# RWKV chunk matrices as 64x64 blocks in two quadrants of the array

## The chip, the cores and the metric

The kernel runs on one core of one Trainium2 chip. The metric is the device time of one execution in microseconds, the median of several runs. One program computes the whole network.

## The reference, cut to what matters

Four layers follow each other: an RG-LRU layer and a sparse-attention layer, each with an MLP, and then, in `second_block`, a layer with differential attention and RWKV-7 side by side and a retention layer, each with two SwiGLU blocks. There are 512 tokens of 1024 features. The change is in the RWKV-7 half of the third layer: eight heads of 64, a recurrence over the tokens.

```
def rwkv7_recurrence(r, w, k, v, kk, a):
    def step(state, inp):
        r_t, w_t, k_t, v_t, kk_t, a_t = inp
        sa = jnp.einsum('bhvk,bhk->bhv', state, -kk_t)
        state = (state * w_t[:, :, None, :]
                 + sa[..., None] * (kk_t * a_t)[:, :, None, :]
                 + v_t[..., None] * k_t[:, :, None, :])
        return state, jnp.einsum('bhvk,bhk->bhv', state, r_t)
```

The result is normalised by head, a bonus `sum(r*k*r_k) * v` is added, and the sum is gated.

## The kernel before, in words

The tokens are cut into 8 chunks of 64. In a chunk the recurrence is a 64x64 triangular system per head. The kernel works on pairs of heads, p = 0 to 3 (128 features, two heads h of 64 rows). Every engine runs its own fixed list of instructions (`rwkv_pe`, `rwkv_act`, `rwkv_pool`, `rwkv_dve`); they meet at counting semaphores. A `Steps` object names the steps of one pair: `done` counts one up, `wait` waits for a named step of pair p. `fr_*` are the steps of the front of a pair, `bk_*` those of its back.

The work of a pair, in order. **Front elementwise work** (`dve_front_0` to `dve_front_7`, `act_front_*`, and the full-width matmuls kk, w, a, g and bonus of 512 columns) makes decayed keys and queries. It is done for pair p+1 between the levels of pair p. **Turns**: four transposes by TensorE, 128x128 each, times four tensors. **Matrices** (`pe_mats`, `dve_mats`): five products of 64 rows deep per head, masked by VectorE on the way out of PSUM. A tile of 128x128 holds two chunks; only its two diagonal 64x64 blocks are in use, the mask clears the others. Four tiles j make the 8 chunks, so each matrix is 128x512. **Levels** (`pe_level_u`, `pe_level_d`): the triangular matrix is inverted by doubling, in five levels l. The matrix D and its transpose DT are both kept. In each level, for each head, U = Gb'D (line 2096), ScalarE copies U out of PSUM (line 2293), then DT'U and U'DT (lines 2109 and 2110), and VectorE adds them to D and DT (lines 2447 and 2448). GpSimd prepares the masked Gb for the next level (line 2350). In level 5 only DT is still wanted. **Back** (`pe_back`): P = DT'RHS, copied out by ScalarE (head 0) and VectorE (head 1, line 2462), then the products QT, Y1, MT and N. **Scan** (`pe_scan`): seven steps that carry the state from chunk to chunk; each waits for VectorE's add of the step before (line 2480). **Normalisation**: VectorE adds the scan's part (line 2488), mean (line 2167), subtraction (line 2495), square on ScalarE (line 2321), variance (line 2172), logarithm and exponential on ScalarE (lines 2323 and 2325), and three elementwise steps on VectorE (lines 2499 to 2501). The matrices of the next pair are made around these.

After the normalisation VectorE scales the next pair's keys (`dve_front_0`, line 2366) and ScalarE squares them (line 2231). In ScalarE's list this square stands ahead of the first U copy of the new pair. In the last pair no front work is left; the first output matmuls (`pe_out_part`, lines 304 to 306) are put between the steps of its scan.

## Time and profile before

| | before |
|---|---|
| median of 3 runs | 3835.3 us (3829.93 to 3839.46) |
| the profiled execution | 3837.58 us, of which the span is 3835.7 us |
| TensorE matmul busy | 3623.7 us, 94% of the span |
| VectorE busy | 1989.1 us, 52% |
| ScalarE busy | 1228.4 us, 32% |
| GpSimd busy | 532.7 us, 14% |
| granted TensorE clock, mean | 0.975 |
| RWKV stage | about 1926 to 2205 us of the span |

A float32 matmul appears in the trace as two records, and its weight load as two; counts of records are therefore twice those of the program's matmuls. A row that says "x16" is 16 records. The duration in a row is that of a record from start to modelled end, so the pace of a stream is read from the starts. A clock of 1.00 is 2.4 GHz, 0.50 is 1.2 GHz.

### The profile page before, as it was taken

The numbers are of one execution on the slowest core, as the hardware profiler recorded it, in microseconds if no ns is written. First come the engines' busy times: TensorE is split into PE (matmuls) and PEld (weight loads), VectorE is DVE, ScalarE is ACT, GpSimd is POOL, SyncE is SP. The second block draws the span as 40 slices with busy tenths as digits, with TensorE's granted clock in tenths as the row PEclk, the third lists the DMA queues.
The fourth block names the chain that finished last, engine by engine and source line by source line (L and its number), as shares of the span: only waits on it lengthen the run. The fifth ranks groups of instructions, "written<-read, shape, count | busy, mean of one in ns | idle before, by whom it ended". The sixth has DMA issues, their size and how long they took to land.

```text
span 3835.7 us, 44975 instructions
## 1 busy us (share of the span) xinstructions
PE 3623.7 (94%) x17279; PEld 2899.5 (76%) x17279; DVE 1989.1 (52%) x2747; ACT 1228.4 (32%) x1651; POOL 532.7 (14%) x398
## 2 busy tenths in 40 slices
PE   6999999899999999998998889999999899989998
PEld 5788888546888788876777768887888677767887
DVE  6555563464555554455566444446444433345445
ACT  3632232464322322233223132224222322233222
POOL 1220010010000221110132121112111100012111
PEclk8999999899999999999999999999999999989999
DMA  3233234001232232221200023232223222222231
GB/s 103 86 102 105 91 95 106 20 1 34 88 104 93 86 97 92 98 87 45 72 12 1 1 77 99 98 98 68 97 98 98 77 77 80 85 66 79 97 98 66
DMA packets 232517, 295.37 MB, mean 77 GB/s; under 512 B 21893, under 2 KB 201464, under 8 KB 232392
## 3 DMA queue, kind: packets, MB, share of 16 engines
q1 hardware_dynamic: 230864, 290.48, 24.0%
q0 software_dynamic: 1152, 3.05, 0.4%
q8 instruction: 85, 1.39, 0.2%
q14 instruction: 40, 0.33, 0.0%
q10 hardware_dynamic: 376, 0.12, 0.0%
HBM read 291.53 MB, written 2.10 MB: 77 GB/s over the span
## 4 chain that ended last, share of the span: by engine, by line
PE 82%; DVE 8%; ACT 4%; POOL 3%; issue 2%; POOLq 0%; ACTq 0%; DMA 0%; DVEq 0%
PE bank L304 23%; PE bank L306 22%; PE bank L305 22%; POOL tmp L636 1%; PE bank L333 1%; PE bank L335 1%; PE bank L334 1%; PE bank L2074 1%; ACT h_hi L550 1%; PE bank L2579 1%; PE bank L2110 1%; DVE x L681 1%; ACT whi L294 1%; DVE wlo L300 1%; DVE h_lo L665 1%
## 5 line engine op out<-in xcount | busy, mean ns | idle before, releaser
L304 PE MATMUL bank<-h_hi,whi 128*128 128x512 f32 x2800 | 1114.3, 398 | 57.2 <-DVE h_lo L665 38.2
L305 PE MATMUL bank<-h_lo,whi 128*128 128x512 f32 x2800 | 1101.8, 393 | 0.0
L306 PE MATMUL bank<-h_hi,wlo 128*128 128x512 f32 x2800 | 1101.4, 393 | 0.0
L294 ACT ACTIVATE whi<-raw 128x2048 fp32r<-128x2048 f32 x273 | 521.7, 1911 | 1400.6 <-PE bank L306 1346.1
L300 DVE TENSOR_TENSOR wlo<-raw,whi 128x2048 fp32r<-128x2048 f32 x273 | 631.9, 2315 | 435.1 <-ACT whi L294 434.8
L304 PEld LDWEIGHTS bank<-h_hi,whi 128*128 128x128 f32 x2800 | 533.8, 191 | 183.0 <-issue 64.0
L305 PEld LDWEIGHTS bank<-h_lo,whi 128*128 128x128 f32 x2800 | 533.7, 191 | 115.5 <-issue 4.9
L306 PEld LDWEIGHTS bank<-h_hi,wlo 128*128 128x128 f32 x2800 | 532.9, 190 | 112.6
L304 PE MATMUL bank<-u_hi,whi 128*128 128x512 f32 x1376 | 539.4, 392 | 27.0 <-DVE wlo L300 10.6
L305 PE MATMUL bank<-u_lo,whi 128*128 128x512 f32 x1376 | 538.2, 391 | 0.0
L306 PE MATMUL bank<-u_hi,wlo 128*128 128x512 f32 x1376 | 538.1, 391 | 0.0
L304 PEld LDWEIGHTS bank<-u_hi,whi 128*128 128x128 f32 x1376 | 260.3, 189 | 85.1 <-DVE wlo L300 11.4
L445 POOL TENSOR_TENSOR tmp<-tmp,rstd 128x512 f32<-128x512 f32 x88 | 175.5, 2015 | 1065.3 <-ACT tmp L414 1065.0
L305 PEld LDWEIGHTS bank<-u_lo,whi 128*128 128x128 f32 x1376 | 260.3, 189 | 54.1
L306 PEld LDWEIGHTS bank<-u_hi,wlo 128*128 128x128 f32 x1376 | 260.0, 189 | 54.3
L499 DVE TENSOR_TENSOR fsum<-fsum,bank 128x512 f32<-128x512 f32 x352 | 235.5, 686 | 92.6 <-PE bank L306 92.5
L499 DVE TENSOR_TENSOR x<-x,bank 128x512 f32<-128x512 f32 x256 | 169.6, 684 | 51.0 <-PE bank L306 50.9
L480 DVE TENSOR_TENSOR tmp<-bank,tmp 128x512 f32<-128x512 f32 x88 | 60.9, 692 | 253.1 <-PE bank L306 236.3
L465 DVE TENSOR_TENSOR tmp<-bank,rstd 128x512 f32<-128x512 f32 x88 | 60.1, 691 | 216.3 <-PE bank L306 215.4
L422 ACT ACTIVATE u_hi<-tmp 128x512 fp32r<-128x512 f32 x88 | 55.7, 633 | 336.5 <-DVE tmp L480 336.5
L469 DVE SCALAR_TENSOR_TENSOR tmp<-bank,rstd 128x512 f32<-128x512 f32 x64 | 44.1, 692 | 180.8 <-PE bank L306 180.8
L426 ACT ACTIVATE tmp<-tmp 128x512 f32<-128x512 f32 x64 | 40.4, 632 | 257.2 <-DVE tmp L469 257.2
(400 smaller groups left out, 3381.2 us busy)
## 6 DMA issues: line engine op xcount, KB each, us to landing
raw<-in_ffn_wgu SPq DMA_DIRECT2D x88, 1024.0 KB, 5.1
raw<-in_ffn_wd SPq DMA_DIRECT2D x44, 1024.0 KB, 4.9
raw<-in_mlp_w_up SPq DMA_DIRECT2D x32, 1024.0 KB, 5.7
raw<-in_mlp_w_down SPq DMA_DIRECT2D x32, 1024.0 KB, 4.9
raw<-in_odd_w_in SPq DMA_DIRECT2D x24, 1024.0 KB, 5.1
raw<-in_even_w_in SPq DMA_DIRECT2D x13, 1024.0 KB, 5.3
raw<-in_rg_w_in SPq DMA_DIRECT2D x8, 1024.0 KB, 5.8
raw<-in_odd_w_out SPq DMA_DIRECT2D x8, 1024.0 KB, 5.0
```

Of the source, the lines that this page charges most:

```text
L294: e.activation(whi[:, n % 2, :], raw[:, n % 2, :], ACT.Copy).then_inc(hi_ready, 1)
L300: e.tensor_tensor(wlo[:, n % 2, :], raw[:, n % 2, :], whi[:, n % 2, :].bitcast(F32), ALU.subtract).then_inc(lo_ready, 1)
L304: pe.matmul(o, w_hi, r_hi, start=first, stop=False)
L305: pe.matmul(o, w_hi, r_lo, start=False, stop=False)
L306: return pe.matmul(o, w_lo, r_hi, start=False, stop=last)
L422: e.activation(u_hi[:, u, :], tmp[:, 2 + j, :], ACT.Copy).then_inc(uhi_done, 1)
L426: e.activation(tmp[:, 2 + j, :], tmp[:, j, :], ACT.Square)
L445: e.tensor_tensor(tmp[:, j, :], tmp[:, j, :], rstd[:, :], ALU.mult).then_inc(scaled, 1)
L465: ins = e.tensor_tensor(tmp[:, j, :], pbank[half + j][:, :], rstd[:, :], ALU.mult)
L469: ins = e.scalar_tensor_tensor(tmp[:, j, :], pbank[half + j][:, :], 0.0, rstd[:, :], ALU.max, ALU.mult)
L480: e.tensor_tensor(tmp[:, 2 + j, :], pbank[half + 2 + j][:, :], tmp[:, j, :], ALU.mult)\
L499: e.tensor_tensor(dst[:, m, :], dst[:, m, :], pbank[half + m % 4][:, :], ALU.add)\
```

## The change

The two diagonal blocks of each 128x128 tile become two matmuls of 64x64, one on rows 0 to 63 of the array with results on partitions 0 to 63 (even chunk), one on rows 64 to 127 with results on partitions 64 to 127 (odd chunk). They sit in two opposite quadrants of the array and alternate. All matrices shrink from 128x512 to 128x256, masks to 64 columns (`m_half`, cut out of the old masks once by GpSimd). `pe_mats` now works in three groups: for each chunk both heads, into one bank per head, so that all four quadrants are used; a group is signalled once. `dve_mats` takes two matrices with one instruction where they lie side by side (`m02`, `m13`). In a level, DT'U and U'DT are no longer interleaved: the one goes to banks 3 and 4 and signals D, the other goes to banks 1 and 5 and signals T; VectorE adds each after its own signal. U goes to banks 0 and 2. In `pe_back` the products QT, Y1, MT and N alternate quadrants; those of odd and even chunks land in different banks, so some copies are done in halves (`odd_even`). The scan's outputs move from bank 6 to bank 5. GpSimd now adds the identity to both heads' D before it prepares the first Gb.

```diff
+        MBANK = ((0, 2), (3, 4), (1, 7))
...
-        def hz(h, j):
-            return rz[:, 11 * h + j, :].rearrange("p (j n) -> p j n", j=QT)
-
-        MATS = [[hz(h, j) for j in range(4)] for h in HH]
-        Dm, DTm, Um, Gb, RHS, PM = ([hz(h, j) for h in HH] for j in range(5, 11))
+        def hz(h, t):
+            return rz[:, 6 * h + t, :]
+
+        def by_chunk(m):
+            return m.rearrange("p (j n) -> p j n", n=HD)
+
+        def two(t):
+            return [[by_chunk(hz(h, t)[:, i * 4 * HD:i * 4 * HD + 4 * HD]) for h in HH] for i in range(2)]
+        (M0, M2), (M1, M3), (Dm, DTm), (Um, Gb) = (two(t) for t in range(4))
+        RHS, PM = ([hz(h, t).rearrange("p (j n) -> p j n", j=QT) for h in HH] for t in (4, 5))
         QTt, MTt = rz[:, 22, :], rz[:, 23, :]
+        EE = (slice(0, HD), slice(HD, P))
...
-        def pe_mats(pe, p, k0, k1):
-            for k in range(k0, k1):
-                i, h = MORD[k]
-                r = slice(h * HD, h * HD + HD)
+        def pe_mats(pe, p, g):
+            if g == 0:
+                fr_dve.wait(pe, "tokA", p)
+                fr_act.wait(pe, "tokB", p)
+            elif g == 1:
+                fr_act.wait(pe, "tokK", p)
+                fr_dve.wait(pe, "tokV", p)
+            else:
+                fr_dve.wait(pe, "bon", p)
+            for s, i in enumerate(MGRP[g]):
                 l_, r_ = ((be, al), (be, rt_of(p)), (kt_, al), (kt_, rt_of(p)), (al, be))[i]
-                b = MBANK[k % 5]
-                if k == 0:
-                    fr_dve.wait(pe, "tokA", p)
-                elif k == 1:
-                    fr_act.wait(pe, "tokB", p)
-                elif k == 2:
-                    fr_act.wait(pe, "tokK", p)
-                elif k == 3:
-                    fr_dve.wait(pe, "tokV", p)
-                elif k == 4:
-                    fr_dve.wait(pe, "bon", p)
-                else:
-                    i0, h0 = MORD[k - 5]
-                    fr_dve.wait(pe, f"d{h0}" if i0 == 0 else f"m{i0}{h0}", p)
-                for j in range(QT):
-                    q = slice(j * P, j * P + P)
-                    ins = pe.matmul(pbank[b][:, q], l_[r, q], r_[r, q], start=True, stop=True)
-                fr_pe.done(ins, f"m{i}{h}")
+                for c in range(8):
+                    q = slice(c * HD, c * HD + HD)
+                    o_ = slice((4 * s + c // 2) * HD, (4 * s + c // 2) * HD + HD)
+                    for h in HH:
+                        ins = pe.matmul(pbank[MBANK[g][h]][EE[c % 2], o_], l_[EE[h], q], r_[EE[h], q], start=True, stop=True)
+            fr_pe.done(ins, f"M{g}")
...
         def pe_level_u(pe, p, l):
             for h in HH:
                 if l == 1:
                     fr_pool.wait(pe, f"gb1{h}", p)
-                    fr_dve.wait(pe, "m31", p)
                 else:
                     bk_pool.wait(pe, f"gb{l}{h}", p)
                     bk_dve.wait(pe, f"D{l - 1}{h}", p)
-                for j in range(QT):
-                    ins = pe.matmul(pbank[h][:, j * P:j * P + P], Gb[h][:, j, :], Dm[h][:, j, :], start=True, stop=True)
+                for c in range(8):
+                    e, j = EE[c % 2], c // 2
+                    ins = pe.matmul(pbank[2 * h][e, j * HD:j * HD + HD], Gb[h][e, j, :], Dm[h][e, j, :], start=True, stop=True)
                 bk_pe.done(ins, f"U{l}{h}")
 
         def pe_level_d(pe, p, l):
             for h in HH:
                 if l == 1:
                     fr_pool.wait(pe, f"DT{h}", p)
+                    fr_dve.wait(pe, "m131", p)
                     if p:
                         bk_act.wait(pe, "yln", p - 1)
+                else:
+                    bk_dve.wait(pe, f"T{l - 1}{h}", p)
                 bk_act.wait(pe, f"U{l}{h}", p)
-                for j in range(QT):
-                    q = slice(j * P, j * P + P)
-                    if l < 5:
-                        pe.matmul(pbank[2 + h][:, q], DTm[h][:, j, :], Um[h][:, j, :], start=True, stop=True)
-                    ins = pe.matmul(pbank[4 + h][:, q], Um[h][:, j, :], DTm[h][:, j, :], start=True, stop=True)
-                bk_pe.done(ins, f"D{l}{h}")
+                for i, (l_, r_) in enumerate(((DTm, Um), (Um, DTm))):
+                    if i == 0 and l == 5:
+                        continue
+                    for c in range(8):
+                        e, j = EE[c % 2], c // 2
+                        ins = pe.matmul(pbank[((3, 4), (1, 5))[i][h]][e, j * HD:j * HD + HD], l_[h][e, j, :],
+                                        r_[h][e, j, :], start=True, stop=True)
+                    bk_pe.done(ins, f"{'DT'[i]}{l}{h}")
...
         def pe_back(pe, p):
             for h in HH:
-                bk_dve.wait(pe, f"D5{h}", p)
+                bk_dve.wait(pe, f"T5{h}", p)
                 fr_act.wait(pe, f"rhs{h}", p)
                 fr_pool.wait(pe, f"ra{h}", p)
-                for j in range(QT):
-                    ins = pe.matmul(pbank[h][:, j * P:j * P + P], DTm[h][:, j, :], RHS[h][:, j, :], start=True, stop=True)
+                for c in range(8):
+                    e, j = EE[c % 2], c // 2
+                    ins = pe.matmul(pbank[h][e, j * P:j * P + P], DTm[h][e, j, :], RHS[h][e, j, :], start=True, stop=True)
                 bk_pe.done(ins, f"P{h}")
             bk_act.wait(pe, "P0", p)
             bk_dve.wait(pe, "P1", p)
-            for h in HH:
-                for j in range(QT):
-                    ins = pe.matmul(pbank[2][h * HD:h * HD + HD, j * P:j * P + P], PM[h][:, j, HD:P],
-                                    MATS[h][1][:, j, :], start=True, stop=True)
+            if p:
+                bk_act.wait(pe, "yln", p - 1)
+            for c in range(8):
+                e, j = EE[c % 2], c // 2
+                for h in HH:
+                    ins = pe.matmul(pbank[(2, 4)[c % 2]][EE[h], c * HD:c * HD + HD], PM[h][e, j, HD:P], M1[h][e, j, :],
+                                    start=True, stop=True)
             bk_pe.done(ins, "QT")
-            for h in HH:
-                for j in range(QT):
-                    o_ = pbank[3][h * HD:h * HD + HD, j * P:j * P + P]
-                    pe.matmul(o_, tokV[:, j, h * HD:h * HD + HD], MATS[h][3][:, j, :], start=True, stop=False)
-                    ins = pe.matmul(o_, PM[h][:, j, 0:HD], MATS[h][1][:, j, :], start=False, stop=True)
+            for c in range(8):
+                e, j = EE[c % 2], c // 2
+                o_ = pbank[(3, 5)[c % 2]][:, c * HD:c * HD + HD]
+                for h in HH:
+                    pe.matmul(o_[EE[h], :], tokV[e, j, EE[h]], M3[h][e, j, :], start=True, stop=False)
+                for h in HH:
+                    ins = pe.matmul(o_[EE[h], :], PM[h][e, j, 0:HD], M1[h][e, j, :], start=False, stop=True)
             bk_pe.done(ins, "Y1")
...
-                        bk_act.done(e.activation(flat(Um[h]), pbank[h][:, :], ACT.Copy), f"U{l}{h}")
+                        bk_act.done(e.activation(flat(Um[h]), pbank[2 * h][:, 0:4 * HD], ACT.Copy), f"U{l}{h}")
...
-                fr_pool.done(e.tensor_tensor(Dm[h], Dm[h], wide(ident[:, :]), ALU.add), f"Dm{h}")
-                fr_dve.wait(e, f"m0{h}", p)
-                fr_pool.done(e.tensor_tensor(Gb[h], MATS[h][0], wide(lmask[:, 1, :]), ALU.mult), f"gb1{h}")
+                fr_pool.done(e.tensor_tensor(Dm[h], Dm[h], wide(ident2), ALU.add), f"Dm{h}")
+            for h in HH:
+                fr_dve.wait(e, f"m02{h}", p)
+                fr_pool.done(e.tensor_tensor(Gb[h], M0[h], wide(low_mask(1)), ALU.mult), f"gb1{h}")
...
-        def dve_mats(e, p, k0, k1):
-            for k in range(k0, k1):
-                i, h = MORD[k]
-                src = pbank[MBANK[k % 5]][:, :].rearrange("p (j n) -> p j n", j=QT)
-                fr_pe.wait(e, f"m{i}{h}", p)
-                if i == 4:
-                    do_fr(e, e.tensor_tensor(Dm[h], src, wide(m_low), MUL), f"m4{h}", p, False)
+        def dve_mats(e, p, g):
+            fr_pe.wait(e, f"M{g}", p)
+            for h in HH:
+                src = by_chunk(pbank[MBANK[g][h]][:, :])
+                if g == 0:
+                    do_fr(e, e.tensor_tensor(Dm[h], src[:, 0:QT, :], wide(m_half[:, 2, :]), MUL), f"m4{h}", p, False)
+                elif g == 1:
+                    do_fr(e, e.tensor_tensor(by_chunk(hz(h, 0)), src, wide(m_half[:, 0, :], 8), MUL), f"m02{h}", p, False)
+                    do_fr(e, e.tensor_tensor(DTm[h], src[:, 0:QT, :], wide(low_mask(0)), MUL), f"d{h}", p, False)
                 else:
-                    do_fr(e, e.tensor_tensor(MATS[h][i], src, wide((m_up, m_upd, m_up, m_upd)[i]), MUL), f"m{i}{h}", p,
-                          False)
-                if i == 0:
-                    do_fr(e, e.tensor_tensor(DTm[h], src, wide(lmask[:, 0, :]), MUL), f"d{h}", p, False)
+                    do_fr(e, e.tensor_tensor(by_chunk(hz(h, 1)), src, wide(m_half[:, 1, :], 8), MUL), f"m13{h}", p, False)
...
-                        bk_pe.wait(e, f"D{l}{h}", p)
                         if l < 5:
-                            e.tensor_tensor(flat(Dm[h]), flat(Dm[h]), pbank[2 + h][:, :], ALU.add)
-                        do_bk(e, e.tensor_tensor(flat(DTm[h]), flat(DTm[h]), pbank[4 + h][:, :], ALU.add), f"D{l}{h}", p,
-                              False)
+                            bk_pe.wait(e, f"D{l}{h}", p)
+                            do_bk(e, e.tensor_tensor(flat(Dm[h]), flat(Dm[h]), pbank[3 + h][:, 0:4 * HD], ALU.add),
+                                  f"D{l}{h}", p, False)
+                        bk_pe.wait(e, f"T{l}{h}", p)
+                        do_bk(e, e.tensor_tensor(flat(DTm[h]), flat(DTm[h]), pbank[(1, 5)[h]][:, 0:4 * HD], ALU.add),
+                              f"T{l}{h}", p, False)
```

On TensorE, one level of the last pair (level 3 and the start of level 4). `L2096` is U, `L2109` is DT'U, `L2110` is U'DT; rz holds all matrices; the last number is partitions x columns of the result. Before:

```order
L2096 MATMUL bank0<-rz_55 128x128 [waits bk_dve,bk_pool]
L2096 MATMUL bank0<-rz_55 128x128 x3
L2096 MATMUL bank1<-rz_55 128x128 [waits bk_dve,bk_pool]
L2096 MATMUL bank1<-rz_55 128x128 x3
L2109 MATMUL bank2<-rz_55 128x128 [waits bk_act]
L2110 MATMUL bank4<-rz_55 128x128
L2109 MATMUL bank2<-rz_55 128x128
L2110 MATMUL bank4<-rz_55 128x128
...
L2109 MATMUL bank3<-rz_55 128x128 [waits bk_act]
L2110 MATMUL bank5<-rz_55 128x128
```

The same level after the change; `L2103` is U, `L2121` both products:

```order
L2103 MATMUL bank0<-rz_55 64x64 [waits bk_dve,bk_pool]
L2103 MATMUL bank0<-rz_55 64x64 x7
L2103 MATMUL bank2<-rz_55 64x64 [waits bk_dve,bk_pool]
L2103 MATMUL bank2<-rz_55 64x64 x7
L2121 MATMUL bank3<-rz_55 64x64 [waits bk_act,bk_dve]
L2121 MATMUL bank3<-rz_55 64x64 x7
L2121 MATMUL bank1<-rz_55 64x64 x8
L2121 MATMUL bank4<-rz_55 64x64 [waits bk_act,bk_dve]
L2121 MATMUL bank4<-rz_55 64x64 x7
L2121 MATMUL bank5<-rz_55 64x64 x8
```

24 matmuls of 128 columns become 48 of 64 columns, in six runs of 8, and the two products of a head stand behind each other instead of alternating.

On VectorE, the adds of the same level and the next. Before, with one wait per head:

```order
L2447 TENSOR_TENSOR rz_55<-rz_55,bank2 128x512 [waits bk_pe]
L2448 TENSOR_TENSOR rz_55<-rz_55,bank4 128x512
L2447 TENSOR_TENSOR rz_55<-rz_55,bank3 128x512 [waits bk_pe]
L2448 TENSOR_TENSOR rz_55<-rz_55,bank5 128x512
L2447 TENSOR_TENSOR rz_55<-rz_55,bank2 128x512 [waits bk_pe]
```

After the change:

```order
L2467 TENSOR_TENSOR rz_55<-rz_55,bank3 128x256 [waits bk_pe]
L2470 TENSOR_TENSOR rz_55<-rz_55,bank1 128x256 [waits bk_pe]
L2467 TENSOR_TENSOR rz_55<-rz_55,bank4 128x256 [waits bk_pe]
L2470 TENSOR_TENSOR rz_55<-rz_55,bank5 128x256 [waits bk_pe]
L2467 TENSOR_TENSOR rz_55<-rz_55,bank3 128x256 [waits bk_pe]
```

The four adds stay in their order; each has half the columns and waits for its own product.

## Rows read from the trace of the kernel before

**Rows 1.** The page: the chain that ended last, share of the span by engine.
```profile
PE 82%; DVE 8%; ACT 4%; POOL 3%; issue 2%; POOLq 0%; ACTq 0%; DMA 0%; DVEq 0%
```
**Rows 2.** Busy by stretch: PE, PEld, DVE, ACT, POOL, then clock, DMA share, GB/s.
```profile
1929.50:2205.00 275.50, 245.97 (x2307) 212.10 (x2306) 160.54 (x278) 72.09 (x130) 76.17 (x64) 0.98 0.01 4
```
**Rows 3.** One level of the last pair, 2144 to 2151, in order of time.
```profile
2144.43 0.69 DVE L2447 TENSOR_TENSOR rz<-rz,bank 128x512 f32<-128x512 f32 x1 [3.10 <-PE bank L2110]
...
2146.01 1.06 PE L2096 MATMUL bank<-rz 128*128 128x128 f32 x8
2146.22 0.69 DVE L2447 TENSOR_TENSOR rz<-rz,bank 128x512 f32<-128x512 f32 x1 [0.50 <-PE bank L2110]
2146.82 0.68 DVE L2448 TENSOR_TENSOR rz<-rz,bank 128x512 f32<-128x512 f32 x1
2147.11 0.60 ACT L2293 ACTIVATE rz<-bank 128x512 f32<-128x512 f32 x1 [3.87 <-PE bank L2096]
...
2147.65 1.13 PE L2096 MATMUL bank<-rz 128*128 128x128 f32 x8 [0.58 <-DVE rz L2448]
...
2150.60 0.69 DVE L2447 TENSOR_TENSOR rz<-rz,bank 128x512 f32<-128x512 f32 x1 [3.10 <-PE bank L2110]
```
**Rows 4.** Quadrant matmuls of the back (L2138) and one scan step.
```profile
1977.93 0.69 PE L2138 MATMUL bank<-fsum,rz 64*64 64x64 f32 x32
...
1981.74 0.34 PE L2161 MATMUL bank<-tmp,rz 64*64 64x64 f32 x4
1981.91 0.29 PE L2162 MATMUL bank<-rz,tmp 64*64 64x64 f32 x4
```
**Rows 5.** VectorE and ScalarE durations by width.
```profile
L2480 DVE TENSOR_TENSOR tmp<-bank,tmp 128x64 f32<-128x64 f32 x24 | 5.4, 225 | 24.4 <-PE bank L2162 23.9
...
1999.64 0.38 ACT L2277 ACTIVATE rz<-bank 128x256 f32<-128x256 f32 x1 [3.11 <-PE bank L2083]
```
**Rows 6.** Second pair: start of level 2, of P, VectorE's front work, end of scan.
```profile
2009.48 2.05 PE L2096 MATMUL bank<-rz 128*128 128x128 f32 x16
...
2034.20 2.05 PE L2119 MATMUL bank<-rz 128*128 128x128 f32 x16
...
2024.62 1.29 DVE L2378 TENSOR_SCALAR tmp<-tmp 128x512 f32<-128x512 f32 x1
...
2027.21 1.58 DVE L2380 TENSOR_TENSOR tmp<-tmp 128x512 f32<-128x512 f32 x1
...
2050.49 0.62 DVE L2488 TENSOR_TENSOR tmp<-tmp,bank 128x448 f32<-128x448 f32 x1 [0.43 <-PE bank L2162]
```
**Rows 7.** From the end of the first pair's scan to the second pair's first level.
```profile
1986.62 0.62 DVE L2488 TENSOR_TENSOR tmp<-tmp,bank 128x448 f32<-128x448 f32 x1 [0.43 <-PE bank L2162]
...
1995.18 0.69 ACT L2323 ACTIVATE tmp<-bank,eps 128x512 f32<-128x512 f32 x1 [2.99 <-PE bank L2172]
1995.90 0.63 ACT L2325 ACTIVATE tmp<-tmp 128x512 f32<-128x512 f32 x1
...
1999.22 0.74 DVE L2499 SCALAR_TENSOR_TENSOR tmp<-tmp,par 128x512 f32<-128x512 f32 x1
...
2001.51 1.58 DVE L2366 TENSOR_SCALAR tmp<-arena,par 128x512 f32<-128x512 f32 x1
...
2003.80 1.12 PE L2007 MATMUL bank<-tmp,arena 128*128 128x512 f32 x2 [1.46 <-ACT tmp L2231]
```
**Rows 8.** Groups by line and shape: VectorE's masked copies of the matrices.
```profile
L2423 DVE TENSOR_TENSOR rz<-bank,arena 128x512 f32<-128x512 f32 x32 | 21.1, 687 | 5.9 <-PE bank L2074 5.8
```
**Rows 9.** Granted clock around the fall in the last pair's scan.
```profile
2160.00:2170.00 10.00, 7.92 (x157) 6.80 (x154) 3.33 (x12) 4.88 (x10) 0.00 (x0) 0.96 0.02 4
2170.00:2175.00 5.00, 3.97 (x21) 2.69 (x22) 0.82 (x2) 0.00 (x0) 0.00 (x0) 0.50 0.00 0
...
2180.00:2185.00 5.00, 3.22 (x19) 2.42 (x20) 1.43 (x4) 0.00 (x0) 0.00 (x0) 1.00 0.00 0
```
**Rows 10.** Scan steps of the last pair at either clock (VectorE's add).
```profile
2170.85 0.23 DVE L2480 TENSOR_TENSOR tmp<-bank,tmp 128x64 f32<-128x64 f32 x1 [2.87 <-PE bank L2162]
...
2175.40 0.23 DVE L2480 TENSOR_TENSOR tmp<-bank,tmp 128x64 f32<-128x64 f32 x1 [3.73 <-PE bank L2162]
...
2182.82 0.22 DVE L2480 TENSOR_TENSOR tmp<-bank,tmp 128x64 f32<-128x64 f32 x1 [2.21 <-PE bank L2162]
...
2185.86 0.23 DVE L2480 TENSOR_TENSOR tmp<-bank,tmp 128x64 f32<-128x64 f32 x1 [2.22 <-PE bank L2162]
```

107 lines of the change are left out of this document (58 added, 49 removed).

## The prediction

> **What bounds the kernel now.** The chain that ended last is to be read first: 82% of it is TensorE [rows 1]. But most of that is the big projections, which the change leaves alone. What counts is the RWKV stage, 275.5 us long [rows 2]. There TensorE shows 246 us busy at a clock of 0.98, VectorE 161, ScalarE 72 and GpSimd 76. So the stage is bound by TensorE, with waits in between, and nobody else is near.
>
> Then the order of time within one level [rows 3]. The first head's add to D comes at 2144.43 and again at 2150.60: a level of the last pair, which has no front work beside it, takes 6.17 us. TensorE's stream fills it: a run of 8 records (4 matmuls of 128 columns) starts every 0.89 us if nothing stands between (8 times 0.112), and a level has six such runs, 5.35 us. The rest is the wait of the second U for VectorE's add (idle 0.58). The reader is to see that ScalarE's copy of U has long idled (3.87 us) when its matmuls come.
>
> **What a run of eight 64x64 matmuls costs.** The trace has such matmuls. In the back, 32 records in four quadrants take 0.69 us to the modelled end of the last [rows 4]; less the 0.22 of that last one, they start within 0.47 us. That is 8 per quadrant, 0.058 us apart. Two opposite quadrants, with results in one bank, are what the scan uses: each head's matmul has its own half of rows and of partitions. Its 4 records take 0.34 us to the end and the next group starts 0.17 us after them [rows 4]. One after the other in a single file they would start over 3 times 0.058, 0.17 us, and end at 0.40; in two quadrants they start over 0.12 and end at 0.34. So they run side by side. A run of 8 matmuls has 16 records, 8 per quadrant: 0.47 us instead of 0.89. The bounds: 0.47, if pairs run side by side, and 0.94 if they don't. I take 0.47.
>
> The row shows two opposite quadrants writing one bank together. The Trainium skill, page "TensorEngine Tiling (Array Packing)", section "Gotcha 1: PSUM Pressure", says that different row tiles cannot access the same PSUM bank simultaneously. By that rule a run would be 0.94 us and the levels would gain nothing on TensorE; the scan's rows speak against it.
>
> **VectorE, ScalarE, GpSimd.** A VectorE instruction of 64 columns takes 0.225 us [rows 5], one of 512 columns 0.687 [rows 8]: 1.03 ns a column. So 256 columns take 0.42, and follow each other every 0.34 instead of every 0.60 [rows 3]. ScalarE's copy of 256 columns takes 0.38 [rows 5] instead of 0.60. GpSimd's instructions halve too; with 76 us busy in the stage [rows 2] I cost them at nothing, hidden beside TensorE's runs, and if that cover went they would add at most 0.7 us a level.
>
> **The sum at full clock, by stage.**
> (a) A level without front work. U starts; its result is with ScalarE 0.67 us later (0.41 for the last start, 0.22 to its end, 0.04 to hand over); the copy takes 0.38 and TensorE starts 0.34 after it (an estimate; the wait behind VectorE in [rows 3], from 2147.50, the end of its add, to 2147.65, is 0.15 and the low end, which would give 3.1); then come four runs, 1.88. Sum 3.3 instead of 6.17, 2.9 less. VectorE's four adds (1.4 us) fit in. Last pair, levels 2 to 5: 4 times 2.9, 11.6.
> (b) Levels 2 to 5 with front work, up to P. Before, 2009.48 to 2034.20, 24.7 us [rows 6]. After: level 2 has six runs and a full-width matmul, 2.8 and 0.86, so 3.7; level 3 the same; behind level 3 VectorE makes the decays, from 2024.62 to 2028.79, 4.2 us [rows 6], and with four adds (1.4) this is 5.6, longer than TensorE's part, so VectorE sets level 4; level 5 has four runs and hand-overs, 3.7. Sum 16.7, 8.0 less, three times: 24.
> (c) From the end of the scan to level 2 of the next pair. Before, 1986.62 to 2009.48, 22.9 us [rows 6, 7], with the matrices in between. VectorE's part of these shrinks from 12 instructions at 0.60, 7.2 us, to 4 at 0.60 and 4 at 0.34, 3.8 us; TensorE's from 80 records at 0.112, 9.0 us, to 160 records in four quadrants at 0.0146, 2.3 us. What is left is a chain that nothing shortens: y and mean 2.2 (0.62, a 512-column matmul 1.12 [rows 7], hand-overs), subtraction, square and variance 2.9, logarithm and exponential (0.69 [rows 7] and about as much) 1.9, three elementwise steps of 0.74 [rows 7] 2.4, the scaling of the next keys 1.58 [rows 7] and 0.1, the square 0.7, the first U copy with hand-over 0.7, four runs 1.9, the matmul w 0.9. Sum 15.3, 7.6 less, three times: 23. The stall moves: before, TensorE waits 1.46 us for the square (L2231) [rows 7]; now it has its matrices early and waits some 5 us there.
> (d) P to the end of the scan: 2034.20 to 2050.49, 16.3 us [rows 6]. QT and Y1 fall from 48 records at 0.112 to 96 records in four quadrants at 0.0146, from 5.4 to 1.4 us, but VectorE's front work (10 instructions of 0.6 behind the last add) then holds P's copy and QT's add: I take 2 less, bounds 0 and 4.0. Three times 6, and 3 in the last pair.
> (e) The first pair's matrices and level 1, by (a) and (c): 3.4 on VectorE, rhs 0.9, level 1 2.9: 7.
> Sum 11.6 + 24 + 23 + 9 + 7 = 75 us.
>
> **The clock.** In the last pair's scan the engine does a few 64x64 matmuls and six 512-column ones per step and waits between; from 2170 the clock is 0.50, by 2180 1.00 again [rows 9]. A step takes 4.55 us at the low level (2170.85 to 2175.40) and 3.04 at the high one (2182.82 to 2185.86) [rows 10]. The changed kernel thins out its work the same way in three places of every pair: the 5 us hole of (c), the hole of some 2 us where VectorE makes the decays, and all levels, in which now one half of the array at most is at work. At the low level six runs take 5.6 us instead of 2.8, so a level 2.7 us more. I count two and a half such levels a pair in the first three, 20 us, and 5 in the last: 25. Bounds: 0 if the clock holds, 100 if it never rises (below). Net 75 - 25 = 50: against the profiled execution 3837.6 - 50 = 3788. That run lies 2.3 above the median of those shown, so I say 3786.
>
> On this the Trainium skill, page "TensorE: Matmul & The Clock Gate", section "What's actually happening", says that the throttled state is the default and that activity releases it. Idle stretches before a fall are what [rows 9] show too; by the rule alone the holes of (c) would bring the low level in every pair, which is why the forecast counts it and the clock that holds is a rival.
>
> **Rivals.**
> The clock holds. For it: through the earlier scans, with 64x64 matmuls between transposes, the stage's mean stayed at 0.98 [rows 2]. Time 3837.6 - 75 = 3763. Chance 0.22.
> Opposite quadrants with one bank go one after the other, the rule above. Levels, rhs and P then stay as they are on TensorE; VectorE's shorter instructions, the matrices and QT, Y1 leave about 35 at full clock (7.6 and 2 three times, 7), less some 12 for the clock: 3815. For it only that the scan's groups are short (two matmuls a head), so that it may show less than it seems. Chance 0.1.
> Slower: the low clock stays through the stage. TensorE streams at full clock some 32 us in a pair of about 46 (28 runs of 0.47, P 1.7, matrices and the back 5.1, transposes 3.4, seven 512-column matmuls 6, scan 1.6). Doubled, that adds up to 32 less what hides beside VectorE's chains, 25 a pair: 100 in all against 75. Time 3863; it decides from 75 us of clock cost on. Against it: each back and each scan has full-width transposes and dense quadrants, after which the clock would rise. Chance 0.06.
> Nothing to measure: several gains fall behind chains that I read too short. 3835, chance 0.06.
>
> **How the numbers follow.** The forecast, the clock low for part of each pair, has 0.56 and its own range 3768 to 3808. The whole range, 3756 to 3820, takes in the clock that holds and the single file; the two last cases are outside. A measurement here can tell about 0.3%, 11.5 us, from no change. Faster by more: 0.56, 0.22, 0.1 and a little of the rest, 0.9. Within: 0.04. Slower: 0.06.
>
> **What the next profile would show.** Right: L2103 and L2121 in runs of 16 records that start within 0.47 us at clock 1.00 (0.94 proves the single file); DVE adds of 0.42 us; levels of the last pair 3.3 us apart at full clock; an idle of TensorE of about 5 us for the square's line; in the stage a mean clock of 0.75 to 0.9. A clock near 0.98 there means 3763; one near 0.6 means that the gain is gone. The prediction is wrong if the stage (275.5 us) is not 215 to 240 us long.

## The result, and the profile after

The changed kernel takes 3767.7 us (median of 4 runs, 3767.1 to 3770.4), the kernel before 3832.6 (median of 4): ratio 0.9829, 95% interval 0.9812 to 0.9846, or 65 us less. The forecast was 3786 with a range of 3756 to 3820. So the direction held, the time lies in the range, and the gain is 15 to 20 us larger than forecast. The profiled executions compare 3835.7 with 3766.3 us of span, 69.4 less.

All of it comes from the RWKV stage. The two ends that can be found in both traces are VectorE's first copy of transposed keys (L2409 before, L2429 after) and the last pair's y (L2488, L2512). Of before:

```profile
1927.51 1.28 DVE L2409 COPY fsum<-bank 128x512 f32<-128x512 f32 x2
...
2188.75 0.62 DVE L2488 TENSOR_TENSOR tmp<-tmp,bank 128x448 f32<-128x448 f32 x1 [2.07 <-PE bank L2162]
```

and of the changed kernel:

```profile
1931.80 1.28 DVE L2429 COPY fsum<-bank 128x512 f32<-128x512 f32 x2
...
2119.49 0.62 DVE L2512 TENSOR_TENSOR tmp<-tmp,bank 128x448 f32<-128x448 f32 x1 [2.08 <-PE bank L2179]
```

261.2 us have become 187.7, that is 73.5 less. From y to the end of the span it is 1646.9 against 1646.8 us. The missing 4.3 us lie ahead of the stage, in code that the change doesn't touch: there the stage begins 4.3 us later. In the twelve further profiles below it begins anywhere from 1928.3 to 1936.6. So 4.3 us is within the spread from execution to execution; but there is only one profile of the kernel before, and it begins earlier than all the others, so that the change has no part in it is not shown.

The busy time of that stretch (windows: PE, PEld, DVE, ACT, POOL, then the granted clock), before and after, to be held against [rows 2]:

```profile
1927.50:2188.80 261.30, 233.09 (x2256) 201.97 (x2254) 156.60 (x274) 69.22 (x125) 76.17 (x64) 0.98 0.02 5
```
```profile
1931.80:2119.50 187.70, 152.13 (x3790) 119.96 (x3790) 117.59 (x262) 59.81 (x129) 50.86 (x64) 0.95 0.03 8
```

The chain that ended last keeps its shares ([rows 1] had 82% for TensorE):

```profile
PE 81%; DVE 8%; ACT 4%; POOL 3%; issue 2%; POOLq 0%; ACTq 0%; DMA 0%; DVEq 0%
```

In the stage TensorE's busy time falls by 81 us, VectorE's by 39; the clock is a little lower, 0.95.

A level of the last pair, which has no front work, in order of time (of after, as [rows 3]):

```profile
2082.30 0.42 DVE L2467 TENSOR_TENSOR rz<-rz,bank 128x256 f32<-128x256 f32 x1 [1.29 <-PE bank L2121]
...
2083.47 1.13 PE L2103 MATMUL bank<-rz 64*64 64x64 f32 x32
...
2084.17 0.85 ACT L2311 ACTIVATE rz<-bank 128x256 f32<-128x256 f32 x2 [2.26 <-PE bank L2103]
...
2084.70 2.08 PE L2121 MATMUL bank<-rz 64*64 64x64 f32 x64
2085.42 0.42 DVE L2467 TENSOR_TENSOR rz<-rz,bank 128x256 f32<-128x256 f32 x1 [1.29 <-PE bank L2121]
```

From one D add to the next it is 3.12 us where it was 6.17. Two runs of U, 32 records, show 1.13 us to the end of the last, and four runs of products, 64 records, 2.08; less 0.22 for that last one, a run of 16 records starts within 0.46 to 0.47 us. That is the pace that the forecast took, and not the single file's 0.94.

The second pair (of after, as [rows 6, 7]):

```profile
1973.81 0.62 DVE L2512 TENSOR_TENSOR tmp<-tmp,bank 128x448 f32<-128x448 f32 x1 [0.43 <-PE bank L2179]
...
1980.49 1.10 PE L2103 MATMUL bank<-rz 64*64 64x64 f32 x32
1985.20 2.08 PE L2023 MATMUL bank<-tmp,arena 128*128 128x512 f32 x2 [3.60 <-ACT tmp L2249]
1987.20 2.55 PE L2121 MATMUL bank<-rz 64*64 64x64 f32 x64
...
1990.74 1.15 PE L2103 MATMUL bank<-rz 64*64 64x64 f32 x32
...
2002.97 1.34 PE L2103 MATMUL bank<-rz 64*64 64x64 f32 x32 [0.89 <-DVE rz L2467]
...
2006.05 1.96 PE L2132 MATMUL bank<-rz 64*64 64x128 f32 x32 [0.49 <-DVE rz L2470]
```

End of scan to level 2 is 16.9 us (22.9 before), level 2 to P 15.3 (24.7 before). TensorE has finished the first level's U at 1981.6 and then waits 3.60 us for ScalarE's square (L2249) ahead of the matmul of line 2023: the hole of the forecast, at 3.6 where it said 5.

The granted clock behind that hole, in the levels behind it, in the last pair's scan and in the last pair's levels:

```profile
1984.90:1988.30 3.40, 3.10 (x22) 1.60 (x24) 0.00 (x0) 0.79 (x3) 0.16 (x1) 0.50 0.00 0
...
1988.30:2003.00 14.70, 13.70 (x346) 11.01 (x343) 9.74 (x19) 8.35 (x17) 5.62 (x6) 1.00 0.01 3
...
2097.50:2107.70 10.20, 7.75 (x36) 5.20 (x36) 1.87 (x6) 3.39 (x7) 0.00 (x0) 0.50 0.00 0
...
2077.20:2089.00 11.80, 11.45 (x352) 10.85 (x352) 6.31 (x17) 3.06 (x8) 4.87 (x7) 1.00 0.02 4
```

The clock is low for 3.4 us behind the hole and back at 1.00 in the levels, where TensorE is busy over 90% of the time with half of the array. In the whole stage it is at 0.50 in three such stretches of 3.4 us, two of them behind the hole (second and third pair) and one in the first pair's scan, and in one of 10.2 us in the last pair's scan, which the kernel before has too ([rows 9]). The forecast wanted a stage mean of 0.75 to 0.9 and has 0.95.

### The profile page after: what moved, and what is told of

It is laid out like the page before. It is cut to its first block, busy times and chain, and to the rows that moved or that the text cites. A ratio compares the mean times of both kernels' runs of the same rounds, so it can differ in the third digit from the quotient of the medians.

```text
span 3766.3 us, 48073 instructions
## 1 busy us (share of the span) xinstructions
PE 3548.0 (94%) x18815; PEld 2819.5 (75%) x18815; DVE 1949.7 (52%) x2735; ACT 1218.9 (32%) x1655; POOL 506.6 (13%) x400
## 4 chain that ended last, share of the span: by engine, by line
PE 81%; DVE 8%; ACT 4%; POOL 3%; issue 2%; POOLq 0%; ACTq 0%; DMA 0%; DVEq 0%
PE bank L304 23%; PE bank L306 23%; PE bank L305 23%; POOL tmp L636 1%; PE bank L333 1%; PE bank L335 1%; PE bank L334 1%; ACT h_hi L550 1%; PE bank L2604 1%; PE bank L2121 1%; DVE x L681 1%; ACT whi L294 1%; DVE h_lo L665 1%; DVE wlo L300 1%; PE bank L1281 1%
## 5 line engine op out<-in xcount | busy, mean ns | idle before, releaser
L304 PEld LDWEIGHTS bank<-u_hi,whi 128*128 128x128 f32 x1376 | 260.5, 189 | 84.1 <-DVE wlo L300 10.6
L469 DVE SCALAR_TENSOR_TENSOR tmp<-bank,rstd 128x512 f32<-128x512 f32 x64 | 44.1, 692 | 180.8 <-PE bank L306 180.8
```

The costliest lines, as they stand in the source:

```text
L304: pe.matmul(o, w_hi, r_hi, start=first, stop=False)
L469: ins = e.scalar_tensor_tensor(tmp[:, j, :], pbank[half + j][:, :], 0.0, rstd[:, :], ALU.max, ALU.mult)
```

## The experiments

All are the changed kernel with one edit; in the last three rows, and where long files have the hole filled, edits add up. "Stage" is the time from the first copy to the last pair's y in the profiled execution (187.7 us in the changed kernel). The kernels ran in three groups of four (1, 2, 3 in the table), each beside new runs of the kernel before, whose medians were 3831.3, 3840.5 and 3831.1. So ratios are to be compared across groups, not microseconds; their intervals are 0.0012 to 0.0022 to either side. Where two kernels are closer than that, the reading rests on the stage. The stage comes from one profile each; the kernel that was run again differs by 0.2 us there. But it holds all stretches of low clock, and these move from kernel to kernel, those in the scans too: a difference of a few us in the stage is to be read with them in mind. The order in which matmuls stand in TensorE's list is called the file here; long files are 16 records of one quadrant in a row.

| | group | median, us | ratio | stage, us |
|---|---|---|---|---|
| changed kernel | result | 3767.7 | 0.9829 | 187.7 |
| the same again | 3 | 3765.1 | 0.9825 | 187.9 |
| even chunks first | 1 | 3776.3 | 0.9848 | 198.3 |
| long files | 2 | 3809.0 | 0.9923 | 221.7 |
| long files, hole filled | 3 | 3787.5 | 0.9876 | 206.3 |
| hole filled | 2 | 3769.9 | 0.9815 | 185.8 |
| joint signals | 1 | 3773.8 | 0.9836 | 195.4 |
| one bank, one add | 1 | 3773.5 | 0.9833 | 194.4 |
| matrices head by head | 2 | 3774.7 | 0.9832 | 191.7 |
| square behind U | 1 | 3758.2 | 0.9795 | 180.8 |
| its matmul later too | 3 | 3753.1 | 0.9792 | 177.5 |
| with the scan's low parts early | 3 | 3747.9 | 0.9773 | 172.2 |
| and fillers ahead of the scans | 2 | 3750.7 | 0.9761 | 170.6 |

The first row again, beside the last group:

> The changed kernel as it is, on the chip of the next three. Every theory: 3768 us, 64 us under the kernel before on the same chip, RWKV stage 188 us from the first transposed copy to the last pair's y.

It came out at 3765.1 us, ratio 0.9825 (0.9805 to 0.9845), with the same three short low stretches and the long one.

**Even chunks first.** Do opposite quadrants work side by side, and does the order of the file matter?

```diff
-                for c in range(8):
+                for c in (0, 2, 4, 6, 1, 3, 5, 7):   # in U's runs and in both products
```

> Only the order of the eight blocks within each run of the levels is changed: even chunks first, then odd ones, so that opposite quadrants no longer alternate. Theory A (the gain of the levels comes from opposite quadrants working side by side): a run of 16 records takes 0.94 us instead of 0.47, a level of the last pair 5.6 us instead of 3.1, about 10 us more in each of the first three pairs and 12 in the last, 3810 us against 3768. Rival B (the gain comes from narrower instructions on VectorE and ScalarE): runs and time stay, 3768. Rival C (thin work lowers the clock): with a quarter of the array at work the granted clock in the levels falls to 0.50 and the time passes 3850.

Measured: 3776.3 us, ratio 0.9848 (0.9832 to 0.9864). The level of the last pair is 3.80 us, neither 3.1 nor 5.6 (VectorE's adds, two levels of the last pair):

```profile
2094.50 0.42 DVE L2467 TENSOR_TENSOR rz<-rz,bank 128x256 f32<-128x256 f32 x1 [1.65 <-PE bank L2121]
...
2098.30 0.42 DVE L2467 TENSOR_TENSOR rz<-rz,bank 128x256 f32<-128x256 f32 x1 [1.65 <-PE bank L2121]
```

The records tell why. These are the starts of U's matmuls (us behind 2092), from where the stream of head 0 is under way:

```
.223 .281 .287 .340 .394 .398 .452 .456 .511 .569 .575 .627
```

One quadrant takes a new record every 0.058 us. The other quadrant's stream begins while three records of the first are still to come (pairs such as .281/.287, .394/.398, .452/.456), so each half run begins 0.287 us behind the last, five records and not eight. A run takes 0.575 us: six of them are 0.65 more than 6 times 0.467, and the level has grown by 0.68. So TensorE starts matmuls of another quadrant beside the ones ahead of them, here some three records deep. Theory A is right in kind (the order decides, at unchanged widths), but not at its price of 0.94 us a run; B falls. The clock in the last pair's levels is 1.00, so C falls too:

```profile
2088.00:2102.00 14.00, 14.00 (x356) 13.71 (x354) 6.09 (x16) 3.07 (x8) 5.08 (x8) 1.00 0.01 4
...
1985.50:1992.30 6.80, 5.40 (x54) 3.89 (x55) 1.53 (x3) 1.18 (x3) 1.27 (x2) 0.50 0.00 0
```

The second line shows the stretch of low clock at the second pair's hole: 6.8 us, where the changed kernel has 3.4. From level 2 to P the four pairs are 1.8, 1.8, 1.8 and 2.6 us longer, 8 of the 10.6 us that the stage has grown by.

**Long files.** That reading was put to the test with 16 records of one quadrant in a row.

```diff
-                for i, (l_, r_) in enumerate(((DTm, Um), (Um, DTm))):
-                    for c in range(8):
+                for odd in range(2):
+                    for i, (l_, r_) in enumerate(((DTm, Um), (Um, DTm))):
+                        for c in range(odd, 8, 2):
```

> In the products of a head all even chunks of both products come first (16 records in one quadrant), then all odd ones; U's runs as in the kernel with even chunks first. In that kernel the odd half of a run began 0.287 us, five records, after the even half, so about three records of another quadrant start beside the stream. Theory A (order decides how much runs side by side, and that reach is short): a head's products take some 1.7 us instead of 0.93, levels of the last pair 4.9 us apart, 3790 to 3800 us. Rival B (the reach is long, or the order does not matter): as with the shorter file, levels 3.8 apart, 3776.

Measured: 3809.0 us, ratio 0.9923 (0.9911 to 0.9935), slower than theory A said. The levels of the last pair are 4.52 us apart (4.9 expected), which gives A its first half. Where T's odd file ends (line 2122) and the next U's even file begins (line 2103), the starts are (us behind 2119):

```
.648 L2122  .707 L2122  .713 L2103  .765 L2122  .819 L2103  .823 L2122  .878 L2103  .882 L2122 (the last)
```

Three records of U have started before T's last one, and a file of 16 follows the one before by 0.754 us, 13 times 0.058: the same three records. The rest is the clock. The windows in the second pair's levels, behind them, in the third pair's levels, and in the last pair's:

```profile
1990.40:2014.30 23.90, 23.75 (x200) 17.92 (x200) 4.57 (x10) 4.88 (x12) 2.91 (x5) 0.50 0.01 1
2014.30:2026.00 11.70, 11.66 (x239) 11.02 (x240) 9.00 (x17) 5.66 (x12) 2.33 (x2) 1.00 0.01 1
...
2051.80:2072.30 20.50, 20.50 (x195) 16.48 (x194) 4.57 (x10) 2.81 (x6) 1.72 (x3) 0.50 0.01 2
2110.70:2127.00 16.30, 16.30 (x358) 15.91 (x356) 6.15 (x15) 3.07 (x8) 4.22 (x6) 1.00 0.01 3
```

In the second and third pair the clock is 0.50 for 23.9 and 20.5 us while TensorE is busy 99 to 100% of the time; in the last pair, with the same levels, it is 1.00. What is different is what stood ahead of them: in the second and third pair the hole of the square, in the last pair none, since it has no front work. In the first pair, where TensorE waits only 0.67 us for the square, the clock is 1.00 in the levels too.

**The hole filled,** in the changed kernel and in the one with long files. The filler's result is overwritten and read by nobody.

```diff
+            fr_act.wait(pe, "rhs1", p - 1)
+            for _ in range(3):
+                pe.matmul(pbank[6][:, :], bones, wa_up, start=True, stop=True)
             fr_act.wait(pe, "sq", p)
-            if p:
-                fr_act.wait(pe, "rhs0", p - 1)
```

> Three full matmuls of 512 columns whose result nobody reads stand ahead of TensorE's wait for the square, so its hole of 3.6 us is filled for 2.6. Nothing else is moved. Theory A (the idle hole brings the low clock behind it, and it costs about half its 3.4 us): clock 1.00 through level 1 in all pairs, 1.7 us less in each pair that had the low stretch, 3764 us. Rival B (the clock falls anyway, by how little of the array the levels use): no change, 3768. Rival C (the filler delays what stands behind it): 3771.

> The kernel with the long files (one quadrant at work for 16 records), and in it the three full matmuls ahead of the wait for the square. With long files the clock was 0.50 for 23.9 and 20.5 us from that hole on, although TensorE was busy 99% of that time. Theory A (the idle hole brings the low level, and levels with one quadrant at work don't bring it back up, but don't bring it down either): the levels run at 1.00 as in the last pair, some 20 us less than with long files, 3789 us. Rival B (one quadrant at work brings the clock down by itself): low stretches of 10 us and more stay in the levels, 3800 to 3809.

With the hole filled the changed kernel takes 3769.9 us, ratio 0.9815 (0.9797 to 0.9832): by the time alone this is unclear. By the trace theory A holds in its place. TensorE's rows in the second pair (the filler is line 2022), and the clock there:

```profile
1988.17 2.84 PE L2022 MATMUL bank<-arena 128*128 128x512 f32 x6
1991.80 1.12 PE L2024 MATMUL bank<-tmp,arena 128*128 128x512 f32 x2 [0.79 <-ACT tmp L2250]
1992.85 2.08 PE L2122 MATMUL bank<-rz 64*64 64x64 f32 x64
...
1995.92 1.15 PE L2104 MATMUL bank<-rz 64*64 64x64 f32 x32
...
1985.00:1996.00 11.00, 10.21 (x152) 5.92 (x144) 7.98 (x14) 3.04 (x7) 6.43 (x8) 1.00 0.01 3
```

From y (1980.41) to level 2 it is 15.5 us where it was 16.9; the stretch behind the hole is gone in both pairs. It gives 1.5 us in each. The stage is only 1.9 us shorter, since in the first pair, whose hole was 1.1 us, the filler costs 1.4 us, and since a new stretch of 3.4 us stands in the third pair's scan, while the last pair's scan has 6.8 instead of 10.2.

In the kernel with long files the same three matmuls give far more: 3787.5 us, ratio 0.9876 (0.9856 to 0.9896) after 0.9923, some 18 us, and 15.4 us of the stage. Theory A said 3789. The two pairs with the long low stretches, from y to y, are 10.1 and 9.8 us shorter, and the first pair is 3.8 longer. The window of the second pair's levels, to be held against the 0.50 above:

```profile
1990.00:2014.00 24.00, 23.55 (x369) 18.65 (x368) 11.96 (x23) 9.71 (x20) 8.06 (x9) 1.00 0.01 2
```

So levels with one quadrant at work did not bring the clock down here; but once a hole had, they did not bring it up either, for 20 us. In the levels of the changed kernel, with two quadrants at work, it was up again after 3.4 us.

With the hole filled in both, the stage is 206.3 us with long files and 185.8 with alternating ones. So alternating in the levels is worth some 20 us of the stage, and the kernel with long files still lies 55 us under the 261.2 of before. No run separates what narrower VectorE, ScalarE and GpSimd instructions give in that from what the matrices and the back gain in four quadrants.

**Signals and banks.** First D's add waits for T's run, and the next U for both adds.

```diff
-                    bk_dve.wait(pe, f"D{l - 1}{h}", p)
+                    bk_dve.wait(pe, f"T{l - 1}{h}", p)
...
-                            bk_pe.wait(e, f"D{l}{h}", p)
+                            bk_pe.wait(e, f"T{l}{h}", p)
```

> D's add waits for the transposed product as well, and the next U waits for both adds: no signal and no add apart, banks as they are. Theory A (the separate signals matter in every level, since a head's next U needs only D): the second head's U waits for two adds after its last product, 0.22 + 2 times 0.42 + 0.1 less the 0.47 of the first U, some 0.7 us more a level, 3780 us. Rival B (it is hidden behind TensorE's other runs): 3768, levels of the last pair still 3.1 apart.

Then D and T of a head in one bank with one add.

```diff
-                        ins = pe.matmul(pbank[((3, 4), (1, 5))[i][h]][e, j * HD:j * HD + HD], ...
+                        ins = pe.matmul(pbank[3 + h][e, (4 * i + j) * HD:(4 * i + j) * HD + HD], ...
...
+                        do_bk(e, e.tensor_tensor(hz(h, 2)[:, o:8 * HD], hz(h, 2)[:, o:8 * HD],
+                                                 pbank[3 + h][:, o:8 * HD], ALU.add), f"T{l}{h}", p, False)
```

> D and its transpose of a head share one bank and are added with one VectorE instruction of 512 columns behind one signal. Theory A: the add takes 0.69 instead of two of 0.42, so the second U waits about 0.5 us a level, less than with two joined adds: 3776 us. Rival B (VectorE's time is what counts, 0.60 in place of 0.68 a head): as fast as apart, 3768 or a little under.

Joint: 3773.8 us, ratio 0.9836 (0.9819 to 0.9852). One add: 3773.5, 0.9833 (0.9815 to 0.9851). The ratios can't tell either from the changed kernel; the stage can, with 7.7 and 6.7 us more. U's two runs in the last pair, in the joint kernel and with one add:

```profile
2086.38 0.68 PE L2103 MATMUL bank<-rz 64*64 64x64 f32 x16
...
2087.31 0.68 PE L2103 MATMUL bank<-rz 64*64 64x64 f32 x16 [0.25 <-DVE rz L2470]
...
2089.86 0.68 PE L2103 MATMUL bank<-rz 64*64 64x64 f32 x16
```
```profile
2083.95 0.68 PE L2103 MATMUL bank<-rz 64*64 64x64 f32 x16
...
2084.89 0.68 PE L2103 MATMUL bank<-rz 64*64 64x64 f32 x16 [0.25 <-DVE rz L2467]
...
2087.37 0.68 PE L2103 MATMUL bank<-rz 64*64 64x64 f32 x16
```

In both the second head's U waits 0.25 us for VectorE's add (in the changed kernel both runs are one row, without a wait). A level takes 3.48 and 3.42 us instead of 3.12. So theory A is right in kind in both, at 0.3 to 0.4 us a level where it said 0.7 and 0.5. From level 2 to P this adds up over the four pairs to 4.2 and 3.3 us; much of the rest of the 7.7 and 6.7 goes with a lower clock (0.92 as the mean of the stage in both, for 0.95). The joint kernel has D and T in banks of their own and is no faster than the one with a shared bank, so it is the separate signal that counts here. D and T in one bank with adds apart was not tried.

**The matrices head by head.** 

```diff
-                for c in range(8):
-                    for h in HH:
+                for h, c in [(h, c) for h in HH for c in range(8)]:
```

> Only the order of the matrices' matmuls is changed: head 0's eight blocks, then head 1's, so that two column halves of one row half alternate, instead of all four quadrants. Theory A (two quadrants side by side): 0.029 us a record instead of 0.0146, the matrices 4.7 us a pair instead of 2.3, of which VectorE hides half, 3772 us. Rival B (blocks in the same rows go one after the other): 0.058 a record, 9 us a pair, 3785. Rival C (VectorE's masks set the pace): 3768.

Measured 3774.7 us, ratio 0.9832 (0.9819 to 0.9845): not to be told from the changed kernel; stage 4.0 us longer. The 128 records of lines 2079 and 2080, here and in the changed kernel:

```profile
1979.51 2.74 PE L2079 MATMUL bank<-arena 64*64 64x64 f32 x128
```
```profile
1976.43 2.09 PE L2080 MATMUL bank<-arena 64*64 64x64 f32 x128
```

2.74 less the last one's 0.22 is 0.020 us a record, against 0.0146 with all four quadrants in turn: better than the 0.029 of theory A, and far from B's 0.058. The starts (us behind 1979.5) show both that blocks in the same rows work side by side and why the mean is below 0.029:

```
.119 .126  .178 .184  .236 .243  .294 .301 .307 .314  .353 .359  .411 .414 .418 .420
```

Within a head two records start every 0.058 us, which is theory A's pace. Now and then four start in one such step; that these are the places where one head's blocks follow the other's, three records deep as above, is an inference from the count. The stage's 4.0 us are 0.7 or so a pair for the matrices and, in the second pair, a low stretch of 6.8 us for 3.4.

**The square.** It is put behind the copies of U that it held up.

```diff
-                if p < 3:
-                    act_front_sq(e, p + 1)
                 for l in LEV:
                     ...
+                    if p < 3 and l == 1:
+                        act_front_sq(e, p + 1)
```

(and the matmul of it behind the first level's products).

> ScalarE's square for the next pair is put behind the two copies of the first level's U, and TensorE's matmul of it behind the first level's products. Theory A (that square, and not the data, holds up level 1 and makes TensorE's hole of 3.6 us): level 1 starts some 4 us earlier in three pairs, the hole and the low clock behind it shrink, 3756 us. Rival B (the next pair's front, which now starts no earlier, sets the end of the pair): no change, 3768.

3758.2 us, ratio 0.9795 (0.9776 to 0.9814), an interval that just touches that of the changed kernel; stage 6.9 us shorter: theory A. TensorE in the third pair:

```profile
2024.40 1.10 PE L2103 MATMUL bank<-rz 64*64 64x64 f32 x32
2025.84 2.08 PE L2121 MATMUL bank<-rz 64*64 64x64 f32 x64 [0.34 <-ACT rz L2308]
2029.11 1.12 PE L2023 MATMUL bank<-tmp,arena 128*128 128x512 f32 x2 [1.19 <-ACT tmp L2248]
2030.16 1.12 PE L2031 MATMUL bank<-arena 64*128 64x512 f32 x2
2031.22 0.97 PE L2103 MATMUL bank<-rz 64*64 64x64 f32 x26
```

The products come right behind the U runs, the hole is 1.2 us, and end of scan to level 2 takes 13.5 us instead of 17.0. But level 2 stands behind two full matmuls. The next kernel moves the square's matmul behind the second level's U (and w ahead of it):

> Only the square and its matmul are moved: the square behind the first level's U copies, its matmul behind the second level's U. Theory A (the matmul of the square held up level 2 by some 2 us a pair): 4 to 6 us under the version that moved the square alone (9.6 under the changed kernel), 3753 us. Rival B (what the levels gain is lost to VectorE's front work behind them): as that version, 3758.

3753.1 us, ratio 0.9792 (0.9769 to 0.9814). End of scan to level 2 falls further, to 11.3 us, but level 2 to P grows from 15.3 to 16.7, since the keys' matmuls now stand in the levels; some 0.8 us a pair stay. The stage is 3.3 us shorter, 177.5; 1.7 of that lie in the last pair's scan, where the low stretch is 3.4 us instead of 10.2 for no reason that the edit gives. The ratio can't tell it from the version before. Between A and B, nearer to B.

In the last pair's scan a step of 3.04 us has TensorE waiting for h's low part, which VectorE makes only behind its add (here in the changed kernel):

```profile
2110.51 0.23 DVE L2504 TENSOR_TENSOR tmp<-bank,tmp 128x64 f32<-128x64 f32 x1 [2.21 <-PE bank L2179]
2110.65 0.68 DVE L2450 TENSOR_TENSOR h_lo<-fsum,h_hi 128x512 fp32r<-128x512 f32 x1
...
2111.48 0.47 PE L304 MATMUL bank<-h_hi,whi 128*128 128x512 f32 x1 [1.03 <-DVE h_lo L2450]
...
2113.55 0.23 DVE L2504 TENSOR_TENSOR tmp<-bank,tmp 128x64 f32<-128x64 f32 x1 [2.22 <-PE bank L2179]
```

Made one step earlier, in the version just described:

```diff
                     if p == 3:
-                        dve_low(e, c - 1)
+                        dve_low(e, c)      # and dve_low(e, 0) behind P's copy
```

(ScalarE's first high part moves ahead of its copy of P likewise) and, in the last version, two full matmuls into bank 2 ahead of each scan, behind a wait for VectorE's add to QT.

> Four things at once. The square behind the first level's U copies, and its matmul behind the second level's U; in the last pair the low parts of h are made one scan step earlier; two full matmuls whose result nobody reads before each scan. Theory A (each removes a wait of its own: 10 us for the square, some 2 us a pair more for its matmul, 1 us in each of six scan steps, and less low clock in the scans): 3735 to 3745 us. Rival B (the next pair's front work sets the pair's end): 3755, no better than the square alone.

> The fastest version without its filler matmuls ahead of the scans. Theory A (they keep the clock up in the scans, some 2 us a pair): 6 us slower than with them, 3756 us where the changed kernel has 3768, and low stretches in the scans. Rival B (they hold up the scan as much as they give): equal or faster, 3748.

With the early low parts 3747.9 us, 0.9773 (0.9756 to 0.9791); the last pair, from P to y, falls from 28.5 to 22.6 us, one us in each of six steps. With the fillers too 3750.7 in another group, 0.9761 (0.9745 to 0.9777). VectorE's add in two scan steps of the last version, and its clock over the whole stage:

```profile
2092.31 0.23 DVE L2511 TENSOR_TENSOR tmp<-bank,tmp 128x64 f32<-128x64 f32 x1 [1.15 <-PE bank L2179]
...
2094.28 0.23 DVE L2511 TENSOR_TENSOR tmp<-bank,tmp 128x64 f32<-128x64 f32 x1 [1.15 <-PE bank L2179]
...
1930.00:2102.00 172.00, 153.64 (x3809) 118.42 (x3807) 119.17 (x262) 60.34 (x130) 49.83 (x64) 1.00 0.03 9
```

A step takes 1.97 us, and the clock is 1.00 throughout. Without the fillers the clock is at 0.50 for 3.4 us behind P in the second, third and last pair, as theory A said; but what they give is 1.6 us of the stage and not 6, and the ratios can't tell the two apart. So by the time it is nearer to theory B. That the fillers delay a scan about as much as the clock gives back is one reading; it was not measured by itself. Both versions beat the changed kernel by 0.5 to 0.7%, about 20 to 26 us.

## Why the prediction was right or wrong

- **Bound, and what a run costs: right.** TensorE sets the levels, and a run of 16 records starts within 0.47 us. The bound of 0.94 and the rival of the single file fall. The Trainium skill, page "TensorEngine Tiling (Array Packing)", section "Gotcha 1: PSUM Pressure", says that different row tiles can't access one PSUM bank at the same time. Here opposite quadrants do, at full pace (16 records within 0.47 us); the measurement decides. What comes nearest to a single file is the order: long files took 4.52 us a level.
- **(a) a level without front work, 3.3: right.** Measured 3.12, with the lower of the two hand-overs given (0.15). Level 2 to P in the last pair went from 23.0 to 11.8 us, 11.2 less for 11.6.
- **(b) levels with front work, 24: too small.** 15.3 us from level 2 to P instead of 16.7, 9.4 less three times, 28. The steps of the levels are 4.0, 4.0, 4.2 and 3.1. The one that was mis-sized is the level with the decays: VectorE does take 4.8 us there (D adds 1997.60 to 2002.41), but TensorE has its own part of that level done beside them, so the level costs 4.2 and the last one 3.1, not 5.6 and 3.7.
- **(c) end of scan to level 2, 23: right at full clock.** Measured 5.9, 5.8 and 8.8 less, 20.5; with the 1.5 us that the low clock takes in two of them, 23.5. The hole was 3.6 us. The forecast called this "a chain that nothing shortens"; it is ScalarE's order and not the data that puts the square and its matmul ahead of the first level, and the moved square takes 3.5 us off in each of two pairs. The last of the three terms was 8.8 and not 7.6: that pair has no square to wait for, and its stretch was 19.2 us before and not 22.9.
- **(d) 9 and (e) 7: 7.0 and 6.5.** (d) has a low stretch of 3.4 us in the first pair's scan.
- **The sum** was 75 and came out at 73.5 with the low stretches in it, some 78 without them (1.5 us in each of two pairs, 1.3 in the first pair, whose P to y is 15.1 us for 13.8 in the third). That it is so near is in part luck: (b) gave 4 us more than forecast, and (c), (d) and (e), as measured, 5 less.
- **The clock, 25: the step that failed.** The prediction counted "two and a half such levels a pair in the first three, 20 us, and 5 in the last". Measured, it is some 4 us, and nothing in the last pair, whose scan is slow in both kernels. It went wrong in one assumption: that levels with half of the array at work are thin in the same way as a hole. They held the high level whenever it was there, and came back to it 3.4 us behind a fall. The range was met because it took in the clock that holds, and not by the way that was given the largest chance. The idea was not empty, though: with one quadrant at work a fall lasted 24 and 20 us, and filling the hole gave 15.4 us of the stage where it gave 1.9 in the changed kernel.
- **Net.** 3837.6 less 78, and 4.3 each for the clock and for the later start of the stage, is 3768: the profiled execution. The case that came true is the rival in which the clock holds (3763, given 0.22); the likeliest one's own range, 3768 to 3808, has the profiled execution at its very edge and the median of 3767.7 just outside. By its own last test, a stage of 215 to 240 us from 275.5, the prediction fails: it is 202.
- **Slower, or nothing:** neither had anything for it in any run.

## What to carry to other kernels

Small matmuls in opposite or neighbouring quadrants pay when they alternate in the file; look at the starts of single records, since the order alone was worth 11 us of this stage in short files and, with the hole filled, 20 in long ones. Cost the clock by what stands ahead of thin work, and not by the thin work alone: here idle stretches of 3.2 to 3.6 us had a fall behind them. Ask first which engine's order makes them, since moving one ScalarE instruction and its matmul gave more (6.9 us of the stage) than filling the hole (1.9). When a stage gets shorter, instructions put "out of the way" ahead of the chain come onto it; read each engine's idle time again.

## What was not expected of the hardware

- Matmuls of another quadrant started beside the ones ahead of them in the file, and ahead of the last of these (2119.713 before 2119.882 with long files), about three records deep: a half run of eight began 0.287 us behind the other half, five records of 0.058.
- The clock long kept the level that it had: the same levels with one quadrant at work ran at 0.50 for 23.9 us behind a hole of 3.2 us and at 1.00 without it, TensorE being busy 98 to 100% of the time in both. The Trainium skill, page "TensorE: Matmul & The Clock Gate", section "What's actually happening", has the throttled state as the default that activity releases. The trace agrees in part: in the levels with two quadrants at work the clock was back at 1.00 behind 3.4 us, while in those with one quadrant, the engine busy 99% of the time, it stayed at 0.50 for 23.9 and 20.5 us.
